# Input projections of an RWKV-7 layer on one Trainium2 core: low-rank steps between the large units, modulation blocks spread over them, weights in half units

## The reference, cut to what matters

```python
xx = centred_shift(h)                      # 0.5 * (prev + next) - h, per segment
xr, xw, xk, xv, xa = (h + xx * mu[i] for i in range(5))
r, k, v = xr @ wr, xk @ wk, xv @ wv        # large
tanh(xw @ w1[e]);  xa @ a1[e]              # low-rank, e = 0, 1
sigmoid((h + xx * mu[5]) @ g1)             # low-rank
```

## Time and profile before

| | us |
|---|---|
| median of 3 runs (lowest to highest) | 2208.27 (2204.72 to 2208.61) |
| the profiled execution | 2202.65 |
| its span, first to last instruction | 2200.9 |
| PE busy (share of the span) | 2017.6 (92%) |
| DVE, ACT, POOL busy | 1178.1, 821.7, 407.3 |
| mean granted clock of TensorE | 0.958 |
| the stage `rwkv_inputs` | from 52.6 to 372.7 |

### The profile page before, as it was taken

How to read it: one execution, slowest core, us unless ns; L and a number is a source line. 1 busy time by engine, 2 the same in 40 slices (tenths; PEclk the granted TensorE clock), 3 DMA queues, 4 the chain that set the end, 5 groups by cost and what they waited for, 6 DMA issues and landing times. The chain is left out here.

```text
span 2200.9 us, 52453 instructions
## 1 busy us (share of the span) xinstructions
PE 2017.6 (92%) x22455; PEld 1753.1 (80%) x22455; DVE 1178.1 (54%) x1840; ACT 821.7 (37%) x1350; POOL 407.3 (19%) x411
## 2 busy tenths in 40 slices
PE   5698988799999988699999999998978998999998
PEld 3497977578888887699999999998645577888887
DVE  4634333666666674328767566666586524333333
ACT  2323223455555543216323233234325524422321
POOL 0011111566666662011000000003210010000000
PEclk8899999699999999798999999998989998999999
DMA  9667676001111000421221221211110013332332
GB/s 316 211 201 215 201 217 173 31 28 35 35 35 35 18 11 11 170 63 36 84 77 59 76 77 58 77 58 56 52 38 1 1 58 96 95 111 81 96 113 78
DMA packets 223113, 191.71 MB, mean 87 GB/s; under 512 B 12586, under 2 KB 207796, under 8 KB 222388
## 3 DMA queue, kind: packets, MB, share of 16 engines
q1 hardware_dynamic: 222900, 188.58, 27.9%
HBM read 170.73 MB, written 17.83 MB: 86 GB/s over the span
## 5 line engine op out<-in xcount | busy, mean ns | idle before, releaser
L530 DVE TENSOR_TENSOR ffn_lo<-ffn_raw,ffn_hi 128x1024 fp32r<-128x1024 f32 (+1 forms) x58 | 77.5, 1335 | 195.6 <-ACT ffn_hi L525 195.6
L550 PE MATMUL banks<-mix_hi,proj_hi 128*128 128x386 f32 (+1 forms) x432 | 152.8, 354 | 14.4 <-DVE proj_lo L530 14.4
L550 PE MATMUL banks<-operand_hi,ffn_w_hi 128*128 128x384 f32 x464 | 156.2, 337 | 4.4 <-DVE operand_lo L496 4.4
L550 PE MATMUL banks<-operand_hi,ffn_w_lo 128*128 128x384 f32 x464 | 155.9, 336 | 0.0
L550 PE MATMUL banks<-operand_lo,ffn_w_hi 128*128 128x384 f32 x464 | 155.9, 336 | 0.0
L550 PE MATMUL banks<-mix_hi,proj_lo 128*128 128x386 f32 (+1 forms) x432 | 147.9, 342 | 0.0
L550 PE MATMUL banks<-mix_lo,proj_hi 128*128 128x386 f32 (+1 forms) x432 | 147.8, 342 | 0.0
L550 PE MATMUL banks<-operand_hi,ffn_hi 128*128 128x512 f32 x352 | 138.4, 393 | 5.2 <-DVE operand_lo L496 2.8
L420 POOL TENSOR_TENSOR norm_squares<-norm_squares,norm_x 128x768 f32<-128x768 f32 (+1 forms) x18 | 29.8, 1656 | 588.1 <-ACT norm_x L414 588.1
L550 PE MATMUL banks<-operand_lo,ffn_hi 128*128 128x512 f32 x352 | 137.9, 392 | 0.0
L550 PE MATMUL banks<-operand_hi,ffn_lo 128*128 128x512 f32 x352 | 137.9, 392 | 0.0
(11 more groups left out here) (307 smaller groups left out, 5660.4 us busy)
## 6 DMA issues: line engine op xcount, KB each, us to landing
mod_raw<-in_mod_w SPq DMA_DIRECT2D x96, 512.0 KB, 6.0
ffn_raw<-in_ff_w SPq DMA_DIRECT2D x32, 1024.0 KB, 5.2
ffn_raw<-in_ff_w SPq DMA_DIRECT2D x46, 512.0 KB, 3.8
ffn_raw<-in_ff_w SPq DMA_DIRECT2D x16, 704.0 KB, 4.6
proj_raw<-in_rw_wr SPq DMA_DIRECT2D x8, 512.0 KB, 4.6
proj_raw<-in_rw_wk SPq DMA_DIRECT2D x8, 512.0 KB, 4.5
proj_raw<-in_rw_wv SPq DMA_DIRECT2D x8, 512.0 KB, 4.7
rwkv_out_raw<-in_rw_wo SPq DMA_DIRECT2D x8, 512.0 KB, 4.1
```

What stands on the lines that cost most here:

```text
L530: signal(eng, eng.tensor_tensor(self.lo[s][:, 0:k_tiles, :], self.raw[s][:, 0:k_tiles, :], self.hi[s][:, 0:k_tiles, :].bitcast(F32), ALU.s ...
L550: mm = pe.matmul(out, a, b, start=(first and n == 0), stop=(last and n == 2), skip_group_check=onto)
```

## The change

- The low-rank units become 24 steps, one per channel tile, that stand between the channel tiles of the large units (`low_steps`). Each step has its own mix tile (`low_mix_hi/lo`, one buffer), its own slice of low-rank weights (`low_hi/lo`, two buffers) and two banks of its own for the sums.
- Both mix buffers now serve the large projections in turn; while the units of one run, each makes one tile of the next.
- Weights come in halves of 4 channel tiles (256 KB) through three buffers, and are split in halves.
- The 38 remaining modulation blocks are spread over 23 units, one (behind channel tile 4) or two (behind tiles 1 and 5), in 4 pieces of 256 KB through 4 buffers. Semaphores are shared with `opening`.
- GpSimd's remainders go to DVE. A weight half is loaded once the remainder of the half three before it has been made; SP's order is that of its own loop, below.
- The result of an odd unit is staged in the tile of the hidden sums, that of the last in the shifted tokens. The loads for the next stage are issued before the last store.

```diff
+MOD_DEEP, MOD_PARTS = 4, 4
...
-        mods = Modulation(c, ctx, d, "mod1", 3, batches)
+        mods = Modulation(c, ctx, d, "mod1", MOD_DEEP, batches, MOD_PARTS, mods_before)
...
+        def low_steps(n):
+
+            m, i = n // CT, n % CT
+            tiles = ({0: (), CT - 2: (CT - 3, CT - 2), CT - 1: (CT - 1,)}.get(i, (i - 1,)) if m == 0 else (i,) if m == 1 else
+                     {CT - 2: (CT - 2, CT - 1), CT - 1: ()}.get(i, (i,)))
+            return [(CT * m + k, (3, CT - 1)[-len(tiles):][at]) for at, k in enumerate(tiles)]
+
+        def mods_of(n):
+
+            count = MOD_BLOCKS - MOD_EARLY
+            at = lambda u: min(count, u * count // (UNITS - 1))
+            blocks = [MOD_EARLY + b for b in range(at(n), at(n + 1))]
+            return list(zip(blocks, (4,) if len(blocks) == 1 else (1, 5)))
...
@@ sync @@
+                def load(part):
+                    if part < 2 * UNITS:
+                        need(sp, w_rest, w_at + part - 2 if part > 2 else 0)
...
+                for n in range(UNITS):
+                    m, i = n // CT, n % CT
+                    load(2 * n + 3)
+                    load(2 * n + 4)
+                    load_mods(n + 1)
+                    if i == CT - 1 and m < 2:
+                        load_low(m + 1)
...
+                    sp.wait_ge(evac_lat, n + 1)
+                    sp.wait_ge(evac_ctx, n + 1)
+                    sp.dma_start(dram[m][:, i, :], out(n)).then_inc(kept, 16)
+                sp.wait_ge(kept, 16 * UNITS)
@@ tensor @@
+                def low(step):
+                    m, k = step // CT, step % CT
+                    pe.wait_ge(low_rest, step + 1)
+                    pe.wait_ge(low_mix_rest, step + 1)
...
+                for n in range(UNITS):
+                    m, i, s = n // CT, n % CT, n % 2
+                    need(pe, evac_lat, n - 1)
+                    need(pe, evac_ctx, n - 1)
+                    for k in range(CT):
+                        part, j = 2 * n + k // HALF_K, k % HALF_K
+                        if j == 0:
+                            pe.wait_ge(w_rest, w_at + part + 1)
+                        if i == 0:
+                            pe.wait_ge(mix_rest, CT * m + k + 1)
...
+                        for b, at in mods_of(n):
+                            if at == k:
+                                mod(b)
+                        for step, at in low_steps(n):
+                            if at == k:
+                                low(step)
@@ vector @@
+                neighbours(0)
+                for k in range(CT):
+                    first_mix(k)
+                    if k + 1 < CT:
+                        neighbours(k + 1)
+                    rest_large(0, k)
+                    if k == 1:
+                        subtract(0)
+                    if k == 2:
+                        subtract(1)
+                for n in range(UNITS):
+                    m, i = n // CT, n % CT
+                    subtract(2 * n + 2)
+                    if n < CT:
+                        shift(i)
+                    if m < 2:
+                        mix_large(m + 1, i)
+                    for nth, (step, _) in enumerate(low_steps(n)):
+                        mix(full[1][:], MU_LOW[m], step % CT, mixed_low(n, nth) + 1)
+                        if m < 2 and nth == 0:
+                            rest_large(m + 1, i)
+                        rest_low(n, nth, step)
...
+                    subtract(2 * n + 3)
+                    dve.wait_ge(w_product, w_at + 2 * n + 2)
+                    need(dve, kept, 16 * (n - 1))
...
@@ scalar @@
+                for n in range(UNITS):
+                    m, i = n // CT, n % CT
+                    round_weights(2 * n + 2)
+                    if m < 2:
+                        round_large(m + 1, i)
+                    for nth, (step, _) in enumerate(low_steps(n)):
+                        round_low(n, nth, step)
...
+                    round_weights(2 * n + 3)
...
-            @block.gpsimd
-            def _(pool):
...
```

More of the change, by code:

```diff
@@ L170, in multiply @@
         if slot == 0:
-            need(pe, self.stored, batch - 1)
+            need(pe, self.stored, self.done_batches + batch - 1)
         at = 2 * (MOD_SHARE - 1 - slot)
[L173 to L179, removed]
+        for i in range(self.parts):
+            piece = self.parts * (n - self.first) + i
+            s = piece % self.deep
+            pe.wait_ge(self.loaded[s], 16 * (self.done_loads[s] + piece // self.deep + 1))
+            for j in range(self.tiles):
+                k = self.tiles * i + j
+                column = 32 * (k % 4)
+                mm = pe.matmul(self.bank(batch)[column:column + 32, 0:MOD_W], self.c.cond[:, k, at:at + MOD_ROWS],
+                               self.raw[s][:, j, :], start=(slot == 0 and k < 4),
+                               stop=(self.closes(n) and k >= 4), tile_position=(0, column))
             mm.then_inc(self.product, 1)
     def turn(self, pe, batch):
-        pe.wait_ge(self.copied, batch + 1)
+        pe.wait_ge(self.copied, self.done_batches + batch + 1)
         for q in range(2):
@@ L551, in three_passes, with rwkv_inputs @@
     return mm
-def rwkv_inputs(c, d, a, xx, hidden, full, dram):
+def rwkv_inputs(c, d, a, xx, hidden, full, dram, mods_before):
     nc = c.nc
@@ L578, in rwkv_inputs @@
         large = [d[n][0].rearrange("(k p) e -> p k e", p=P) for n in ("rw_wr", "rw_wk", "rw_wv")]
[L579 to L652, removed]
+        MU_LARGE, MU_LOW = (0, 2, 3), (1, 4, 5)
+        LOW_LOADS = (2, 4, 5)
+        def out(n):
+            return even_out[:] if n % 2 == 0 else hidden[:, 2, :] if n < UNITS - 1 else xx[:, 0, 0:TOK]
+        def low_steps(n):
[3 more added lines that the diff above has]
+            return [(CT * m + k, (3, CT - 1)[-len(tiles):][at]) for at, k in enumerate(tiles)]
@@ L660, in _ @@
             def _(sp):
[L661 to L691, removed]
-                        sp.wait_ge(evac_ctx, CT * m + tile + 1)
-                        sp.dma_start(column(dram[m], tile), out[u.s][:]).then_inc(kept, 16)
@@ L695, in _ @@
[L695 to L703 removed]
+                def load(part):
+                    if part < 2 * UNITS:
+                        need(sp, w_rest, w_at + part - 2 if part > 2 else 0)
+                        n, k = part // 2, HALF_K * (part % 2)
+                        tile = n % CT
+                        sp.dma_start(w_raw[part % 3][:], large[n // CT][:, k:k + HALF_K, tile * P:tile * P + P])                            .then_inc(w_loaded[part % 3], 16)
@@ new lines, in load_low, with load_mods @@
+                def load_low(m):
+                    need(sp, low_rest, CT * m)
+                    if m < 2:
+                        for e in range(2):
+                            sp.dma_start(low_raw[:, :, 64 * e:64 * e + 64], small[m][:, :, e, :]).then_inc(low_loaded, 16)
+                    else:
+                        sp.dma_start(low_raw[:], small[m]).then_inc(low_loaded, 16)
+                def load_mods(n):
+                    for b, _ in mods_of(n) if n < UNITS else []:
+                        for i in range(MOD_PARTS):
+                            mods.load(sp, b, i)
@@ new lines, in keep, with finish_low @@
+                def keep(k):
+                    need(act, mix_rest, k - 1)
+                    nc.scalar.activation(full[k % 2][:], a[:, k, 1:PAD + 1], ACT.Identity, scale=c.par[:, PKEEP + k:PKEEP + k + 1])\
+                        .then_inc(kept_part, 1)
+                def finish_low(m):
+                    act.wait_ge(low_product, CT * (m + 1))
+                    if m == 2:
+                        act.wait_ge(kept, 16 * (UNITS - 2))
+                    f = (ACT.Tanh, ACT.Copy, ACT.Sigmoid)[m]
+                    for b, src, dst, width in PAD_PIECES:
+                        nc.scalar.activation(hidden[:, m, dst:dst + width], c.bank[4 + b][:, src:src + width], f)\
+                            .then_inc(small_copied, 1)
```

305 lines of the change are left out of this document (158 added, 147 removed).

## The result

The changed kernel is slower, by 0.3%. Twenty runs of each gave a median of 2215.43 us (2207.04 to 2218.43) against 2208.47 us (2202.44 to 2212.81): ratio 1.0031, interval 1.0020 to 1.0042. The forecast was 2192.5 with a range to 2206; it missed both the sign and the range. The profiled execution took 2212.13 us, with a span of 2210.4.

What follows compares the result with a forecast made beforehand. TensorE was taken as the bound, with some 30 us lost inside the stage. 4.5 - 1.4 + 2.3 + 8.5 + 8.0 - 2.7 - 0.9 - 0.5 - 2.0 = 15.8 us off 2208.27 gives 2192.5, range 2181 to 2206.

Steps and rivals of the forecast that it cites:

- I count 0 for the pairs: Units with two modulation blocks: the second's last piece lands at 5.5 us, 0.7 to spare, so 0 us lost.
- The slower rival: Second modulation blocks land late, 1.05 us (no change) to 2.3 us (2226 us) in each of 15 pairs; chance 0.11.
- The sign that I named for it: Block matmuls in the stage would show some 15 waits of 1 us or more for their DMA.
- The start: Stage start: earlier weight remainder, in halves, lets PE begin near 60.9 instead of 65.4; 4.5 us won.
- The first unit: First large unit stays bound by DVE's mix chain, lasting 21.2 us; 11.5 lost against 10.1, that is -1.4.
- The second unit: Second large unit: no bunch of blocks delays it; 1.8 of its 4.1 us loss remains, 2.3 won.
- half-weight remainder: DVE's remainder of half the weights, at the start and in each unit, taken as 0.61 us.
- 128 x 128 one: DVE's remainder of the low-rank weights, a shape not in the trace, taken as 0.25 us.
- The two late steps: Low-rank steps not ready at their place: 0.9 us lost in unit 6 and 0.5 in unit 16.
- The end: Stage end: a large unit is last, so its store is exposed; 4.3 us instead of 1.6, costing 2.7.
- the passages: Two passages around a low-rank unit would run at the full stretch's price, winning 8.5 and 8.0 us.
- small waits: All small waits of the stage together, taken as a cost of 2 us.

Runs made afterwards that it cites:

- e1_hold: Changed kernel, with SP holding the store and both weight halves until a unit's second modulation block has landed; 2210.95 us, 1.0020 of the kernel before.
- e5_room: Changed kernel with modulation room for one and a half blocks, in 512 KB pieces through 3 buffers, even results staged elsewhere; 2188.29 us, 0.9925 of the kernel before.
- e6_room_small: Changed kernel with room for one and a half modulation blocks, six buffers of 256 KB, even results staged elsewhere; 2186.72 us, 0.9918 of the kernel before.
- e3_parts2: Changed kernel with modulation blocks in 2 pieces of 512 KB through 2 buffers, same one block of room; 2203.60 us, 0.9975 of the kernel before.

## Why the prediction was wrong, and where it was right

**The step that failed** is "I count 0 for the pairs", in the part on the modulation loads. It let the second block's last piece land 5.5 us after the first block began, by the shortest issue and the shortest landing and with nothing else in flight. The runs put three corrections in its place. The first issue stands 0.66 us behind the block's start, not 0.4, and the issues take 1.90 us together. The store and halves are issued while the block is in flight, which lengthens its last landings: without them the second blocks lose 4.7 us in all and not 24.0 (e1_hold). And when they are held back, the next unit's first block pays. Issue ends 2.56 us after the block's start (109.63 - 107.07); the third piece is waited for until 113.91, 6.84 us after it, 1.3 us later than the whole block was to have landed. The block behind, with 8.2 us from the second block's start (120.67 - 112.48), is in time. Measured cost, where 0 stood: 25.6 us by the waits, and 376.55 - 353.61 = 22.9 by the stage of e5_room, which is without them.

**The slower rival was the true one.** The measured lateness is 25.6 / 15 = 1.7 us, between its 1.05 and its 2.3, and the sum with it is 2208.3 - 15.8 + 25.6 = 2218 (2215 with the 22.9), against 2215.43 measured. That the second agrees so well is luck in part: without the pairs the stage won 19.1 us and not 15.8 (below), and the lower clock behind it and some us of scatter make up for that. I gave it 0.11, on the ground that these loads find an empty queue. They do, but the queue does not stay empty. The sign that I named for it, some 15 waits of 1 us or more, is the one that came, split in two per pair.

**The other steps held.** The start was forecast 4.5 us earlier and is 4.6 (60.77 against 65.4). The first unit, forecast at 21.2 us, lasts 20.1; it is bound by the mixes, at a granted clock of 0.84, but its last six matmuls run at the full clock. It loses 20.14 - 9.66 = 10.5 against 10.1 before, so -0.4 for -1.4. The second unit, forecast to keep 1.8 of its loss, keeps none: 13.2 us at a clock of 1.00 for 11.9 of work (it now has two blocks and a low-rank step), and the 1.3 between them is its second block, late as the others. In e5_room it takes 12.66 (80.85 to 93.51), 0.7 more than its work, which wins 3.4 of the 4.1, where 2.3 were forecast. The half-weight remainder takes 0.69 us and the 128 x 128 one 0.29, where 0.61 and 0.25 were taken; neither is waited for in e5_room behind the first matmul. The two late steps came where they were forecast, in unit 6 (0.8 us for 0.9) and in unit 16 (1.1 for 0.5); the profile puts the second wait down to no engine, but its step starts 0.1 us after its mix remainder ends on DVE:

```profile
PE banks L561 <- DVE low_mix_lo L771: 0.8, 1, 0.8
...
287.21 0.42 PE L561 MATMUL banks<-low_mix_hi,low_rank_hi 128*128 128x386 f32 x1 [1.07 <-issue]
```

In e5_room they are 1.2 and 1.5 us, and the second unit's step adds 0.5:

```profile
PE banks L561 <- DVE low_mix L773: 1.7, 2, 1.2
PE banks L561 <- issue: 1.5, 1, 1.5
```

The end costs 3.4 us from the last projection's matmul to the next stage (376.55 - 373.12) against 1.6, that is 1.8 where 2.7 stood. What I did not price is the lower clock behind that gap, 1.6 us.

The sum of what held can be tested: e5_room has no pair waits, and its next stage starts 372.73 - 353.61 = 19.1 us earlier than that of the kernel before. By its measured parts, 4.7 (start) - 0.4 + 3.4 + 16.5 (the passages, of which no trace is left) - 1.2 - 1.5 (the two steps) - 1.8 = 19.7. The forecast had 15.8, as it took 2.0 for small waits that hardly came, and more for the first unit and the end. The time of e5_room, 18.0 under the median beside it, is in the forecast range: all steps but one held in their mechanism, and their sizes were off by up to 2 us each.

**What stays open.** Behind the stage nothing was changed, yet from the next stage's start to the end of the span the profiled executions took 1828.2 us before (2200.9 - 372.7), 1833.9 after, 1828.1 in e5_room and 1831.6 in e6_room_small. The lower clock at its start is in the last three and can't be the whole of it. I take these up to 6 us for scatter of single executions (the 20 runs of each kernel spread over 10 and 11 us); no run settles it.

## What to carry to other kernels

A buffer that holds one block makes a round trip of every reuse: freed by the use, issued, landed, used. Count it from the use, with the time of every issue, the median landing rather than the shortest, and everything else that the queue sends meanwhile, and compare it with the shortest distance between two uses, not with the mean rate. When a stage is rearranged, look first at whether the buffer that shrank was the one which paid for the uneven spacing; room for half a block more was worth 2207 x (1.0031 - 0.9918) = 25 us here.

## What the runs showed that I had not expected

- Transfers issued later take time from earlier ones. With the store and the weight halves right behind it the second block waited for its third piece; with them held back it was 0.43 us longer than an unhindered one, and the stores landed in 2.8 us and not 5.4.
- The piece size of 256 or 512 KB made no difference to rate or time that can be told once there was room (223 GB/s in both), but with one block of room it made 0.56% (1.0031 against 0.9975).
- After 3.07 us without a matmul the next 16 ran at a granted clock of 0.63 (4.45 us), and in e6_room_small at 0.50 (5.49 us), which is the lower of the two levels (1.2 GHz of 2.4) all the way. In e3_parts2 they took the full-clock 2.85 us after the same pause of 3.08 us:

```profile
366.44 2.85 PE L1721 MATMUL banks<-hidden,mix_full 64*128 64x256 f32 x16 [3.08 <-PEq L635]
```
